# Moving the area of A and of the mixers' tiles by 64 bytes in a two-block kernel

## The reference

```python
def first_block(x, ...):                     # once
    x = x + 0.5 * rms_norm(swiglu(rms_norm(x), f1_in, f1_out))   # 1024 -> 2 x 2816 -> 1024
    h = rms_norm(x)
    q, k, v, u = split(h @ w_mix_in)         # 4 x 512 columns
    mixed = concat([dilated_attention(q, k, v), s5_mixer(u)]) @ w_mix_out
    x = x + rms_norm(mixed)
    return x + 0.5 * rms_norm(swiglu(rms_norm(x), f2_in, f2_out))

def second_block(x, ...):                    # two layers
    for l in range(2):
        x = layer_norm(ALPHA * x + 0.5 * swiglu_2(x, gate1, up1, down1))
        u, q, f, v, g = split(x @ w_in)      # 5 x 512 columns
        y = concat([multiscale_pool(u), head_rms_norm(hgrn2(q, f, v)) * silu(g)])
        x = layer_norm(ALPHA * x + y @ w_out)
        x = layer_norm(ALPHA * x + 0.5 * swiglu_2(x, gate2, up2, down2))
    return x
```

## The kernel before

| Tensors | first byte | modulo 256 |
|---|---|---|
| `X`, `Hh`, `Hl` | 1152, 17536, 33920 | 128 |
| `whi`, `wraw` and `wlo` | 50304, 66688 | 128 |
| `acc`, `zsum`, `Rb`, `MUb`, `tmp0` to `tmp4`, `dgt`, `identr`, `colr`, `sq` | 87040 to 108288 | 0 |
| arena: `Ah`, `Al`, `Y` | 116544, 161600, 206656 | 64 |
| arena, first mixer: `Qf`, `Kf`, `Vt`, `PT`, `U2`, `yh`, `yl`, `Up`, `W1`, `G2`, `Wri` | 116544 to 208704 | 64 |
| arena, second mixers: `QP` and `Ph`, `KS` and `Pl`, `FT`, `TT`, `V2`, `Sc`, `Sg`, `Oh`, `U3`, `PA` | 116544 to 215104 | 64 |

## Time and profile before

### The profile page before, as it was taken

How to read it: one execution, slowest core, us unless ns; L and a number is a source line. 1 busy time by engine, 2 the same in 40 slices (tenths; PEclk the granted TensorE clock), 3 DMA queues, 4 the chain that set the end, 5 groups by cost and what they waited for, 6 DMA issues and landing times.

```text
span 3058.6 us, 32142 instructions
## 1 busy us (share of the span) xinstructions
PE 2973.0 (97%) x13432; PEld 2432.3 (80%) x13432; DVE 1326.0 (43%) x1783; ACT 1002.4 (33%) x1345; POOL 402.9 (13%) x427
## 2 busy tenths in 40 slices
PE   8999989999999999999999999999999999899998
PEld 6888876578888788887887888878888788788886
DVE  5453267545343333334655333343333465543333
ACT  4232234353232232223333332233232333343222
POOL 3110057311110000011231000100001113200010
PEclk9999989799999999999998999999999899899998
DMA  4322212122332232322212333222232221123322
GB/s 137 98 98 92 94 56 69 16 70 91 98 98 93 83 98 98 98 92 76 76 49 67 95 99 98 90 76 96 97 97 92 73 76 49 62 97 97 97 90 75
DMA packets 76016, 260.39 MB, mean 85 GB/s; under 512 B 11728, under 2 KB 11856, under 8 KB 75856
## 3 DMA queue, kind: packets, MB, share of 16 engines
q1 hardware_dynamic: 75872, 258.34, 26.3%
HBM read 255.03 MB, written 2.10 MB: 84 GB/s over the span
## 4 chain that ended last, share of the span: by engine, by line
PE 92%; DVE 5%; issue 1%; ACT 1%; POOL 0%; DMA 0%; SPq 0%; DVEq 0%; POOLq 0%; ACTq 0%
PE bank L324 25%; PE bank L326 25%; PE bank L325 25%; PE bank L338 2%; PE bank L339 2%; PE bank L344 2%; PE bank L435 2%; PE bank L682 2%; PE bank L445 1%; DVE Hl L1290 1%; PE bank L373 1%; PE bank L377 1%; PE bank L374 1%; PE bank L589 1%; PE bank L607 1%
## 5 line engine op out<-in xcount | busy, mean ns | idle before, releaser
L1282 DVE TENSOR_TENSOR wlo<-wraw,whi 128x1024 fp32r<-128x1024 f32 x474 | 588.4, 1253 | 839.3 <-ACT whi L791 838.8
L324 PE MATMUL bank<-Hh,whi 128*128 128x512 f32 x2320 | 910.3, 392 | 11.3 <-DVE wlo L1282 9.6
L325 PE MATMUL bank<-Hh,wlo 128*128 128x512 f32 x2320 | 905.6, 390 | 0.0
L326 PE MATMUL bank<-Hl,whi 128*128 128x512 f32 x2320 | 905.1, 390 | 0.0
L791 ACT ACTIVATE whi<-wraw 128x1024 fp32r<-128x1024 f32 x479 | 499.2, 1055 | 966.3 <-DMA wraw<-weights 966.0
L324 PEld LDWEIGHTS bank<-Hh,whi 128*128 128x128 f32 x2320 | 437.6, 189 | 105.7 <-issue 12.1
L326 PEld LDWEIGHTS bank<-Hl,whi 128*128 128x128 f32 x2320 | 437.1, 188 | 91.8
L325 PEld LDWEIGHTS bank<-Hh,wlo 128*128 128x128 f32 x2320 | 437.3, 189 | 89.6
L324 PE MATMUL bank<-Ah,whi 128*128 128x512 f32 x1056 | 417.1, 395 | 0.0
L326 PE MATMUL bank<-Al,whi 128*128 128x512 f32 x1056 | 416.4, 394 | 0.0
L325 PE MATMUL bank<-Ah,wlo 128*128 128x512 f32 x1056 | 416.2, 394 | 0.0
(11 more groups left out here) (258 smaller groups left out, 2557.6 us busy)
## 6 DMA issues: line engine op xcount, KB each, us to landing
wraw<-weights SPq DMA_DIRECT2D x479, 512.0 KB, 3.4
X<-x_t SPq DMA_DIRECT2D x8, 256.0 KB, 7.3
y_t<-X SPq DMA_DIRECT2D x8, 256.0 KB, 2.0
Y<-masks SPq DMA_DIRECT2D x1, 512.0 KB, 8.5
MUb<-ssm SPq DMA_DIRECT2D x1, 256.0 KB, 7.7
tmp<-ssm SPq DMA_DIRECT2D x1, 256.0 KB, 3.7
zsum<-attention SPq DMA_DIRECT2D x1, 256.0 KB, 4.1
MUb<-attention SPq DMA_DIRECT2D x1, 256.0 KB, 4.1
```

The lines of the kernel that those rows point to most:

```text
L324: pe.matmul(b, sh, mh, start=start, stop=False)
L325: pe.matmul(b, sl, mh, start=False, stop=False)
L326: signal(pe.matmul(b, sh, ml, start=False, stop=stop), keys)
L1282: dve.tensor_tensor(wlo[:, u % NS, :], wraw[:, u % NS, :], f32(whi[:, u % NS, :]), SUB).then_inc(*S.done("weights_lo", ("lo", u)))
```

## The change

One line is added before the arena begins. `top[0]` is 116544 there and `o_w`, the start of `wraw`, 66688; the line adds (66688 - 116544) modulo 256 = 64 bytes. Every tile of the arena then starts 64 bytes later, at 128 modulo 256. No other tile, instruction, wait or transfer is different.

```diff
@@ -222,6 +222,7 @@
     pw = at("pw", [P, 5, 9, 16], F32)
     sp5 = at("sp5", [P, 16, 16], F32)
     M8 = at("M8", [P, 2, 32], F32)
+    top[0] += (o_w - top[0]) % 256
     arena = top[0]
     cur = [arena]
 
```

## The result

| | before | changed |
|---|---|---|
| median of six runs | 3056.15 us (3050.13 to 3058.15) | 3037.12 us (3029.93 to 3042.76) |
| profiled execution | 3060.43 us, span 3058.6 | 3040.53 us, span 3038.7 |
| ratio of the times, 95% interval | | 0.9940 (0.9924 to 0.9956) |

The change makes the kernel 0.6% faster; 3035.0 was forecast, and the span fell by 19.9 us against the 20.9 of the sum. The changed kernel has the same 32142 instructions, and TensorE's matmuls are again busy for 97% of the span. One line was added, so every line number of `mm3` is one higher.

The account below looks back on a forecast made before the run. TensorE's matmul count times their pace, plus breaks at the norms, was taken as the bound. Only moving arena rows gain: 3055.94 - 20.9 = 3035.0 us, all other terms 0; range 3029 to 3042.

Parts of the forecast that it names:

- (a): Moving arena rows in six out stages and the gate product: 1072 tiles save 0.020 us each, 20.9 us after interruptions.
- No change: the step is not of the place: Rival: the arena rows' price comes from region or row-to-weights distance, which 64 bytes leave alone; 3055.9 us, chance 0.08.
- Equal places collide: Rival: high rows starting at the weights' place modulo 256 meet them, 6.7 ns on 3216 matmuls; 3077.4 us, chance 0.04.
- (c): Mixers' float32 matmuls with arena operands: weight load sets their pace whatever the place; 0, with 2 us kept as spread.
- (d): VectorE, ScalarE and GpSimd on arena tiles: zero on the path, even if all 132 became 5 ns slower.
- (e): Weights consumed faster in the out stages, 5.44 us a unit instead of 5.60: cover stays, no new wait for wlo.
- (b): The 24 matmuls with Ph and Pl, most at half clock, where the step is absent: taken as 0.
- (f): Half-clock stretches behind the out stages may grow or shrink: taken as 0, with 3 us kept as spread.
- 3028.3: Time in us of the rival that the mixers' float32 matmuls gain with all of their bound as well; chance 0.02.

Follow-up runs that it names:

- first probe: Changed kernel plus 30 groups of 40 throwaway matmuls at varied distances between row and weights starts, some with fewer weight columns: 9.32 us a group at 0, 9.56 at -64.
- second probe: Changed kernel plus 27 groups of 40 throwaway matmuls varying row length and type: with 512 fp32r columns 9.31 us a group at distance 0, 9.56 at -64.

## Why the prediction was right

- The main term, (a). It was 21.4 us less 0.5. The six out stages and the gate product gave 2 x 3.52 + 4 x 3.44 + 0.31 = 21.1 us, worked out from the first and last starts of each stage. The comparison inside one trace, `Hh` rows against `yh` rows by the same helper, was enough to forecast it; the twist is that the trace before could not tell distance from place. The prediction left that open, and the change brought the same under both.
- "No change: the step is not of the place" was right to be carried and fell: the same high tiles run at 0.680 in the changed kernel, and 256 bytes further too. One argument against it was wrong, though: a price by distance is flat over 90 KB after all, since only the distance modulo 256 counts, and that the 64 bytes do change. "Equal places collide" is the reverse of what happens.
- (c), (d), (e): the 3.48 us of the mixers' 32 float32 matmuls, the 688 ns, and out stages without idle time of TensorE at DMA shares of 0.29 to 0.30 are as forecast. No new wait for `wlo` stands in the out stages.
- (b), the pooled product, was taken at 0. Its 12 matmuls in each layer take 0.8 us less from the first start to the last (1603.90 - 1596.21 = 7.69 us before, 1592.59 - 1585.67 = 6.92 after, and 0.87 less in the second layer). Full clock came back earlier there, with a granted clock of 0.78 in place of 0.68, so this belongs to (f).
- (f) is where the missing 1.2 us (21.1 - 19.9) sits, inside the 3 us that were kept for it; pieces of both signs make it up. The largest piece is the in stage behind the last mixer. The same stretch before and after, in the view of windows:

```profile
2601.50:2911.30 309.80, 301.14 (x1320) 249.23 (x1319) 123.85 (x155) 103.39 (x134) 15.94 (x11) 0.97 0.27 89
```

```profile
2582.80:2894.80 312.00, 303.42 (x1320) 251.12 (x1319) 124.10 (x155) 103.48 (x135) 15.92 (x11) 0.96 0.27 88
```

The same 1320 matmuls take 2.2 us more at a granted clock of 0.96 in place of 0.97. Over the whole span the mean clock stayed at 0.97.
- The offset of 4.5 us between the profiled execution and the median was taken for one of this execution. The profiled 3060.43 us lie 2.3 above the highest of the six runs in the table; but the kernel before reached 3060.30 in another set of 13, the changed kernel's profiled execution lies 3.4 above its own median, and the 3039.5 forecast for a profiled execution met 3040.53. So the offset was one of the execution, as assumed.
- Two figures of the forecast do not follow from its terms. Spreads of 3 and 2 us give 3030 to 3040, not 3029 to 3042, and the cases outside hold 0.14 and not 0.12, since 3028.3 lies outside as well. The 3037.12 lie inside either range.
- One step of my reasoning did not hold, though no term hung on it. I read the pace as the load's 187 ns plus 40 or 47. In the first probe 40 matmuls with 256 columns and loads of 128 columns take 4.87 us without the small matmul's 0.14, 122 ns each, less than the 187 to 192 ns that their loads are shown with. The load's shown duration does not bound the pace, and at distance 0 a shorter load does not shorten the matmul; at -64 it does, by the price of the distance. That the weight load sets the pace of the float32 matmuls in (c) was argued in the same way, and no run shows it; what the runs show is that this pace did not move.
- The Trainium skill's rule that loading the next weights takes nothing from the row's read of the running matmul ("TensorE: Matmul & The Clock Gate", "Step-by-step: what each phase is for") is not what these runs show for fp32r: moving one of the two reads by 4 bytes against the other changes the pace by 9 ns. The rule of the same page of the Trainium skill for back-to-back matmuls, columns at 2.4 GHz plus some 2.5 ns ("Wait — 56ns, not 53.3ns?"), gives 215.8 ns for 512 columns; the bf16 groups agree (8.77 us for 40 and the small matmul's 0.14, 215.8 each), the fp32r stream with 226.7 at its best does not.

Open: what in the memory or the engine the distance acts on; why 512 columns at +64 cost 1.8 ns a matmul in the first probe and 2.3 in the stages, but 6 ns in the second probe, where the group before ran at -64 and not at 48, so that the price is not set by the distance alone; and what the 13.4 ns above the columns' 213.3 are, which no distance removed.

## What to carry to other kernels

Where TensorE streams fp32r rows of 512 columns with a new weight tile of 128 columns for each, let rows and weight tiles start at the same place modulo 256 bytes; being off costs up to 4% of such a matmul (9 of 227 ns) and shows when the starts of consecutive matmuls are subtracted, hardly in mean durations (395 against 392 ns in the earlier trace rows). Compare the pace of one helper over its different operands before blaming the loop around it. And read the trace, not the time alone, when an experiment comes out "the same": two moves of opposite sign gave 3056 here.

## What was not expected

Bytes decide: 4 bytes of distance cost 9 ns a matmul, more than 64 do. In the stages a row above its weights by 64 is cheaper than one below (0.687 and 0.700 us a tile), though the second probe had both alike. One of a tile's three matmuls at -64 costs more than a third of what three cost (0.693 us a tile). The price shrinks with the weight load: 6.0 ns with 128 weight columns, 0.3 with 32. At half clock the effect is absent: a tile takes 1.28 us at distance -64 and at 0, and 1.28 with `Ph` at distance 0 in the changed kernel.
